# Projecting the samples' queries ahead of the prompt in a one-core decoder step with a streamed key and value cache

## What is computed

```python
qkv = rms_norm(x) @ w_in                       # 1024 -> 3072 = 24 tiles of 128 columns
qa, ka, va, qb, kb, vb = split(qkv)            # 4 tiles each; rope on qa, ka, qb, kb
oa = (softmax(q1 k1^T) - lam * softmax(q2 k2^T)) v      # 4 heads, whole past
ob = dilated_window_attention(qb, kb, vb)               # 8 heads, last 2048 positions
x  = x + concat(headnorm(oa), ob) @ w_out
x  = x + (silu(h @ w_gate) * (h @ w_up)) @ w_down       # h = rms_norm(x)
```

## Time and profile before

| | us |
|---|---|
| median of 3 runs | 1069.75 |
| lowest, highest | 1060.89, 1073.51 |
| the profiled execution | 1071.72 |
| its span | 1070.0 |
| PE busy | 948.3 (89%) |
| DVE busy | 667.0 (62%) |
| ACT busy | 516.6 (48%) |
| POOL busy | 287.7 (27%) |
| moved by DMA | 310.99 MB, mean 291 GB/s |

### The profile page before, as it was taken

How to read it: one execution, slowest core, us unless ns; L and a number is a source line. 1 busy time by engine, 2 the same in 40 slices (tenths; PEclk the granted TensorE clock), 3 DMA queues, 4 the chain that set the end, 5 groups by cost and what they waited for, 6 DMA issues and landing times.

```text
span 1070.0 us, 29358 instructions
## 1 busy us (share of the span) xinstructions
PE 948.3 (89%) x11042; PEld 844.3 (79%) x11042; DVE 667.0 (62%) x1632; ACT 516.6 (48%) x1128; POOL 287.7 (27%) x351
## 2 busy tenths in 40 slices
PE   3989999899977888888898568899999999999996
PEld 2978888788855656676676444899999999999996
DVE  5289845676569997863546355888888888700004
ACT  6554433375236468664242653555555555611124
POOL 1322155555433355335454000000000000233330
PEclk8989999999999999998999868999999999999998
DMA  7789999999999999899988974487686876974632
GB/s 227 270 293 327 350 321 378 365 369 374 381 366 385 370 382 347 275 337 337 357 268 265 304 217 161 162 309 279 243 317 261 310 276 233 338 252 161 230 140 89
DMA packets 158229, 310.99 MB, mean 291 GB/s; under 512 B 14049, under 2 KB 88162, under 8 KB 157090
## 3 DMA queue, kind: packets, MB, share of 16 engines
q1 hardware_dynamic: 134242, 233.92, 63.0%
q0 software_dynamic: 22144, 72.37, 19.1%
q10 hardware_dynamic: 1728, 3.15, 0.9%
HBM read 302.31 MB, written 73.92 MB: 352 GB/s over the span
## 4 chain that ended last, share of the span: by engine, by line
PE 38%; issue 32%; DMA 15%; DVE 6%; ACT 5%; POOL 2%; POOLq 1%; ACTq 0%; SPq 0%; DVEq 0%
DMA v_ring<-in_cache_v_diff 12%; PE ps L1477 11%; PE ps L1111 9%; PE ps L1342 5%; PE ps L1305 4%; PE ps L1262 2%; DVE kt_sb L2280 1%; DMA v_ring<-in_state_v_win 1%; ACT rot L1616 1%; POOL v_ring L698 1%; PE ps L1318 1%; PE ps L1359 1%; PE ps L1188 1%; DMA x<-in_x_prompt 1%; DMA k_ring<-in_cache_k_diff 1%
## 5 line engine op out<-in xcount | busy, mean ns | idle before, releaser
L2280 DVE STREAM_TRANSPOSE kt_sb<-k_ring 128x512 f32<-128x512 f32 x336 | 218.7, 688 | 67.7 <-DMA k_ring<-in_cache_k_diff 30.7
L698 POOL DMA_DIRECT2D v_ring<-in_cache_v_diff x248 | 136.3, 551 | 157.6 <-issue 84.5
L1050 POOL TENSOR_TENSOR c_lo<-c_raw,c_hi 128x1408 fp32r<-128x1408 f32 x14 | 46.6, 3331 | 410.7 <-ACT c_hi L1893 410.7
L1111 PE MATMUL ps<-h_hi,w_hi 128*128 128x288 f32 x384 | 124.8, 325 | 1.9 <-DVE h_lo L2134 1.9
L1111 PE MATMUL ps<-h_lo,w_hi 128*128 128x288 f32 x384 | 115.8, 301 | 0.0
L1342 PE MATMUL ps<-v_ring,pt_sb 128*32 128x128 f32 x2240 | 79.2, 283 | 40.8 <-DMA v_ring<-in_cache_v_diff 34.0
L1111 PE MATMUL ps<-h_hi,w_lo 128*128 128x288 f32 x384 | 115.3, 300 | 0.0
L1342 PEld LDWEIGHTS ps<-v_ring,pt_sb 128*32 128x32 f32 x2240 | 61.1, 113 | 53.2 <-issue 49.5
L1305 PE MATMUL ps<-kt_sb,q_st 128*32 128x128 f32 (+1 forms) x2816 | 95.4, 278 | 6.2 <-DVE q_st L2290 4.1
L1006 POOL TENSOR_TENSOR w_lo<-w_raw,w_hi 128x1024 fp32r<-128x1024 f32 x24 | 57.4, 2392 | 153.7 <-ACT w_hi L1594 153.7
L1305 PEld LDWEIGHTS ps<-kt_sb,q_st 128*32 128x32 f32 x2816 | 72.0, 113 | 23.1 <-issue 16.2
(11 more groups left out here) (249 smaller groups left out, 2346.9 us busy)
## 6 DMA issues: line engine op xcount, KB each, us to landing
k_ring<-in_cache_k_diff SPq DMA_DIRECT2D x256, 256.0 KB, 7.1
v_ring<-in_cache_v_diff POOLq DMA_DIRECT2D x248, 256.0 KB, 7.0
out_k_win_sample<-in_state_k_win SPq DMA_DIRECT2D x32, 1020.0 KB, 8.2
out_v_win_sample<-in_state_v_win SPq DMA_DIRECT2D x32, 1020.0 KB, 8.2
k_ring<-in_state_k_win SPq DMA_DIRECT2D x32, 512.0 KB, 6.7
w_raw<-in_w_in SPq DMA_DIRECT2D x24, 512.0 KB, 7.3
g_raw<-in_w_gate SPq DMA_DIRECT2D x11, 1024.0 KB, 5.4
g_raw<-in_w_up SPq DMA_DIRECT2D x11, 1024.0 KB, 5.4
```

The costliest lines, as they stand in the source:

```text
L698: queue.dma_start(dst, src.rearrange("(b j) c -> j b c", b=4))\
L1050: nc.gpsimd.tensor_tensor(c_lo[j][:, 0:width], c_raw[:, j, 0:width], c_hi[j][:, 0:width].bitcast(F32), ALU.subtract).then_inc(w_lo_done, 1)
L1111: last = nc.tensor.matmul(M[c][:, 0:HALF], wt, act[:, k, c * HALF:(c + 1) * HALF], start=k == 0 and at_first, stop=k == KT - 1 and act is ...
L2280: V.transpose(kt_sb[:, i, :], k_ring[:, i, :]).then_inc(kt_done, 1)
```

## The change

- The samples' block is normalised first (`NORM_ORDER = (4, 0, 1, 2, 3)`). ACT copies its transposed rows to a new buffer `h_s` in plain f32, and `project_samples` multiplies the loaded, unsplit tiles 0 to 3 with it: 8 matmuls of 64 columns a tile into one bank. Tile 3 gets a place of its own (`early_raw`), so that four tiles are loaded at the start.
- `copy_sample_queries` (ACT) and `rope_sample_queries` (DVE) make `q_s` of them; `fetch_first_q` and `fetch_q(0)` run at once, between the norms of the blocks. Tiles 0 to 3 have 2 times 256 columns later on in place of 2 times 288, and their rope leaves the samples out.
- `PRE = 0`: every piece of the prompt is in the groups. `SHARE` is 9 a group for groups 0 to 7 (before: 6), 8 for 8 to 21 (as before), 92 pieces in groups 22 to 37 (before 80), and 4 a group for 38 to 47.
- The page numbers are loaded ahead of the weight tiles and are waited for by themselves; the prompt's blocks of x are loaded by ACT's queue. Item 3 uses place 0 with all of `fetch_q(3)` at the end of group 23.
- The four copies of sample 0 go from tiles 0 to 3 into the down projection's loop.
- Some semaphores are merged; what they order stays.

```diff
-PRE = 36
+PRE = 0
-SHARE = [6] * 8 + [8] * 14 + [5] * 20 + [4, 4] + [3] * 4 + [0] * (SLOTS - 48)
+SHARE = ([9] * 8 + [8] * 14 + [6] * 4 + [5] + [6] * 5 + [7] + [5, 5, 6] + [5, 5] + [4] * 10
+         + [0] * (SLOTS - 48))
-    return 0 if it < 3 else it % 2
-FETCH_AT = {23: 3, 30: 4, 33: 5, 36: 6, 39: 7}
+    return 0 if it < 4 else (it + 1) % 2
+FETCH_AT = {30: 4, 33: 5, 36: 6, 39: 7}
@@ SP
-            for blk in range(NBLK):
-                load_x(blk)
...
-            w_in_chunk(0)
-            w_in_chunk(1)
-            w_in_chunk(2)
+            load_x(4)
+            sp.dma_start(g_rows[:, :], ins["norm_attn_g"].partition_broadcast(P)).then_inc(norm_in[0], 16)
+            sp.dma_start(ident[:, :], consts[:, C_ID:C_ID + P]).then_inc(norm_in[0], 16)
+            sp.dma_start(page_ids[:, :], ...).then_inc(norm_in[0], 16)
+            for n in range(4):
+                w_in_chunk(n)
...
+            sp.wait_ge(norm_in[0], 48)
+            for i in range(8):
+                load_keys(0, i)
...
-                    if j == 4 and n < COPIES:
-                        shift_window(*shifts.pop(0))
...
+                if m % 2:
+                    shift_window("k_win", 0, m // 2)
@@ PE
+            def project_samples(n):
+                pe.wait_ge(*landing_of(n))
+                pe.wait_ge(qs_copied, 2)
+                for k in range(KT):
+                    last = nc.tensor.matmul(Z[1][:, n * NS:n * NS + NS], raw_at(n)[:, k * P:k * P + P], h_s[:, k, :],
+                                            start=k == 0, stop=k == KT - 1)
+                last.then_inc(qs_projected, 1)
...
+            norm_transposes(0, NORM_ORDER[0])
+            for n in range(4):
+                project_samples(n)
+            for u in range(1, NBLK):
+                norm_transposes(u, NORM_ORDER[u])
             pe.wait_ge(hlo_done, 2 * NBLK)
-            for p in range(PRE):
-                main(p)
@@ ACT
+            for blk in range(4):
+                act.dma_start(x[0:P, blk, :], x_of(blk)).then_inc(x_in[blk], 16)
+            squares_of(0)
+            norm_root(0, NORM_ORDER[0])
+            act.wait_ge(xn_t, 1)
+            ... (h_s copies)
+            norm_hi(0, NORM_ORDER[0], h_hi)
             split_hi(0)
+            squares_of(1)
+            norm_root(1, NORM_ORDER[1])
+            squares_of(2)
+            norm_root(2, NORM_ORDER[2])
+            copy_sample_queries()
+            squares_of(3)
+            norm_root(3, NORM_ORDER[3])
+            norm_hi(1, NORM_ORDER[1], h_hi)
+            fetch_q(0)
+            squares_of(4)
+            norm_root(4, NORM_ORDER[4])
+            norm_hi(2, NORM_ORDER[2], h_hi)
+            norm_hi(3, NORM_ORDER[3], h_hi)
+            norm_hi(4, NORM_ORDER[4], h_hi)
@@ DVE
+            def rope_sample_queries():
+                dve.wait_ge(const_in, 16 * N_CONST)
+                dve.wait_ge(qs_copied, 4)
+                for f in range(4):
+                    s = slice(f * NS, f * NS + NS)
+                    V.tensor_tensor(feat[:, 1, s], feat[:, 1, s], rope_cs[:, 0, SEQ:NT], ALU.mult)
+                    last = V.tensor_tensor(rot[:, s], rot[:, s], rope_cs[:, 1, SEQ:NT], ALU.mult)
+                last.then_inc(rope_parts, 2)
+                dve.wait_ge(rope_parts, 2)
+                for f in range(4):
+                    V.tensor_tensor(q_s[:, f, :], feat[:, 1, s], rot[:, s], ALU.add).then_inc(rope_s_done, 1)
...
+                rows(2)
+                rope_sample_queries()
+                fetch_first_q()
+                mean(3)
+                low(1)
+                rows(3)
+                mean(4)
+                low(2)
+                rows(4)
+                low(3)
+                low(4)
```

More of the change, by code:

```diff
@@ L855, in load_values @@
                 values_of_group(sp, t, h, first_ids)
-            sp.wait_ge(const_in, 16 * N_CONST)
-            for i in range(8):
-                load_keys(0, i)
             def store_k(n):
@@ L892, in main @@
                 if p < 8 * TILES:
-                    if j == 0 and n and n + 2 < TILES:
+                    if j == 0 and n >= 2 and n + 2 < TILES:
                         w_in_chunk(n + 2)
@@ L1087, in norm_transposes @@
                 pe.wait_ge(xn_done, u + 1)
-                if u < NBLK and blk >= 3:
+                if 3 <= u < NBLK:
                     pe.wait_ge(hlo_done, 2 * (u - 2))
@@ L1419, in turn_output @@
                 nc.tensor.transpose(X[:, 0:P], o_row[:, :], ident[:, :]).then_inc(x_full, 1)
-            pe.wait_ge(norm_in[0], 32)
-            for blk in range(NBLK):
-                norm_transposes(blk, blk)
+            pe.wait_ge(norm_in[0], 48)
+            norm_transposes(0, NORM_ORDER[0])
[3 more added lines that the diff above has]
+                norm_transposes(u, NORM_ORDER[u])
             pe.wait_ge(hlo_done, 2 * NBLK)
-            for p in range(PRE):
-                main(p)
             pe.wait_ge(const_in, 16 * N_CONST)
@@ L1615, in rotate_halves, with copy_sample_queries @@
                     d = slice(32 * (q ^ 1), 32 * (q ^ 1) + 32)
-                    last = nc.scalar.activation(rot[d, :], feat[s, n % 2, :], ACT.Copy)
+                    last = nc.scalar.activation(rot[d, cols], feat[s, n % 2, cols], ACT.Copy)
                 last.then_inc(rot_done, 1)
+            def copy_sample_queries():
+                act.wait_ge(qs_projected, 4)
+                cols = slice(0, 4 * NS)
+                nc.scalar.activation(feat[:, 1, cols], Z[1][:, cols], ACT.Copy).then_inc(qs_copied, 1)
+                act.wait_ge(qs_copied, 3)
+                for q in range(4):
+                    s = slice(32 * q, 32 * q + 32)
+                    d = slice(32 * (q ^ 1), 32 * (q ^ 1) + 32)
+                    last = nc.scalar.activation(rot[d, cols], feat[s, 1, cols], ACT.Copy)
+                last.then_inc(qs_copied, 1)
             def evac_tokens(n):
@@ L1918, in _ @@
                         main(p)
-                    if (t, i) == (0, 2):
-                        fetch_q(0)
-                    if i == 7 and t + 1 in FIRST[1:3]:
+                    if i == 7 and t + 1 in FIRST[1:4]:
                         fetch_q(FIRST.index(t + 1))
@@ L2135, in norm_lo, with mean, rows, low @@
                                     hi[s].bitcast(F32), ALU.subtract).then_inc(hlo_done, 1)
-            def norm_blocks():
-                for blk in range(NBLK):
-                    norm_mean(blk, blk)
-                    if blk:
-                        norm_rows(blk - 1, blk - 1)
-                norm_lo(0, 0, h_hi, h_lo)
-                norm_rows(NBLK - 1, NBLK - 1)
-                for blk in range(1, NBLK):
-                    norm_lo(blk, blk, h_hi, h_lo)
+            def rope_sample_queries():
[8 more added lines that the diff above has]
+                for f in range(4):
+                    s = slice(f * NS, f * NS + NS)
+                    V.tensor_tensor(q_s[:, f, :], feat[:, 1, s], rot[:, s], ALU.add).then_inc(rope_s_done, 1)
+            def norm_blocks():
+                def mean(u):
+                    norm_mean(u, NORM_ORDER[u])
+                def rows(u):
+                    norm_rows(u, NORM_ORDER[u])
+                def low(u):
+                    norm_lo(u, NORM_ORDER[u], h_hi, h_lo)
+                mean(0)
+                dve.wait_ge(norm_in[0], 48)
+                rows(0)
+                low(0)
+                mean(1)
+                rows(1)
+                mean(2)
+                rows(2)
[9 more added lines that the diff above has]
+                low(4)
             def rope(n):
```

142 lines of the change are left out of this document (77 added, 65 removed).

## The result

| | before | changed |
|---|---|---|
| median, us | 1068.8 (4 runs) | 1098.76 (4 runs) |
| lowest, highest | 1060.89, 1073.51 | 1092.96, 1100.14 |
| span of the profiled execution | 1070.0 | 1097.5 |

The ratio is 1.0289, 95% interval 1.0238 to 1.0341: 30 us slower, where 1065 was forecast and 1079 was the upper end.

The account below looks back on a forecast made before the run. Nearly everything is full from 60 to 130 us, DMA to 600, PE alone from 660. At group 8's first scores +13.1 - 12.3 - 8.9, then +3.2 for owed bytes, make -4.9: 1065 us forecast, range 1052 to 1079.

Parts of the forecast that it names:

- the edits costed at nothing: Sample 0's moved copies, item 3's fetch, the list behind group 22, load issues, merged semaphores, last norm: 0 in the sum.
- Term 1: Start: pieces wait for all five blocks and the samples' chain, first piece from 25.63 to about 38.7, +13.1 us.
- The later bound: Start of the pieces at 42.7 if constants and tile 3 come 4 us later than summed.
- The constants: Start: last constants landed at 23.4 us, and DVE's rope of the samples' queries comes after them.
- Terms 2 and 3: Ahead of group 8: fewer and smaller pieces, -12.3 us, and fewer stalls, -8.9 us.
- Twelve pieces fewer: Ahead of group 8's first scores: 75 pieces instead of 87 with PRE = 0, -9.5 us.
- the 9.8 expected: Groups 0 to 7: expected at 9.8 us a group with a DMA share near 0.9.
- the change of item: Among the stalls before group 8: copies and then scores at 125 us, about 2 us, expected to stay.
- Term 4: Full DMA stage from group 8: 1.18 MB of weights and stores still owed, +3.2 us, bounds 0 and 3.8.
- The pace: Groups 8 to 21: expected at 13.2 to 13.4 us a group.
- B: Rival: PE and DVE take turns in groups 0 to 7, stalls stay at 13, +9 us, 1079; chance 0.16.
- C: Rival: bytes set the end, the full stage gives the earlier start all back, sum 0, 1070; chance 0.12.

Follow-up runs that it names:

- e13_list: Kernel before with the changed kernel's list of pieces, keeping its own start, copies and fetches: 1097.2 us, ratio 1.0302.
- e1: Changed kernel with before's list from group 22 on and the 12 pieces put into groups 8 to 19: 1083.4 us, ratio 1.0104.
- e9: Changed kernel with 52 pieces in groups 22 to 29, reaching before's 236 pieces at group 30, then 5 a group: 1082.6 us, ratio 1.0115.
- e8_spread: Changed kernel with its pieces from group 30 on spread evenly, 5 a group and then 4: 1094.1 us, ratio 1.0252.
- e14_ahead: Kernel before with five more pieces done by group 27, so the attention stands one group earlier from 30 to 36: 1077.2 us, ratio 1.0116.
- e16_both: Changed kernel with 60 warming matmuls at the start and a list reaching 236 pieces at group 30: 1086.3 us, ratio 1.0183.
- e7_copies: Kernel before with only sample 0's four copies moved into the down loop: 1067.9 us, ratio 1.0007.
- e4_pre36: Changed kernel with 36 pieces ahead of the groups (PRE = 36) and before's list: 1085.4 us, ratio 1.0141.
- e6_front: Changed kernel with before's list from group 22 and second place, 18 warming matmuls, blocks' transposes between samples' products, rotation and fetches behind norms: 1071.4 us, ratio 1.0037.
- e2_place: Changed kernel with before's list from group 22, 12 pieces in groups 8 to 19, item 3's second place and copies over group 23: 1078.8 us, ratio 1.0103.
- e3_quarter: Changed kernel with the samples' product doing 2 of 8 depth blocks a tile (wrong first queries): 1094.1 us, ratio 1.0224.

## Why the prediction was wrong

**The step that failed** stands under the edits costed at nothing: "From group 22 on the list makes up its 12 pieces over 16 groups, under the same DMA share." Put at 0, it costs half of the loss or more: alone in the kernel before it makes 1.0302, 30 us (e13_list), and taken out of the changed kernel in two ways it gives 15 to 16 us back by the medians, 19 to 20 by the ratios (e1, e9). What the runs show in its place is groups 30 to 36 in 91.3 us instead of 74.6, at a DMA share of 0.77 for 0.95. It rested on a mean DMA share, 0.96 for 440 to 600 us, which seemed to leave PE (135 busy of 160 us) room. That share depended on the pieces' work falling where PE still used the values in time: it is 0.86 in the changed kernel, and in the six groups of e13_list, the kernel before with another list, 0.79 for 0.95. Counting pieces missed it: e8_spread and e14_ahead have before's number a group there and are slow.

**Term 1**, +13.1, was +21.5 (47.12 instead of 25.63). The samples' product ended at 28.6, not 20.8. I read "x12" as 12 matmuls; in plain f32 each is two instructions, so a tile's 8 are 16. I charged only the last tile's and held the others hidden behind the weights, while 64 at 0.213 us outlast the loads by far. The later bound I gave was 42.7. What came behind the product was sized well: 18.5 us to the first piece, where the sum has 17.9. The constants, at 23.4 in the sum, did not matter: DVE's rope waited for ACT until 30.86. (The first key load, issued at 18.6 instead of 23.47, no longer waits for them.) By the Trainium skill, TensorE: Matmul & The Clock Gate, Part 1, the idle state is the throttled one; the trace agrees with its 0.213 us beside a column of 1.00, against 0.112 in e16_both. Over all 64 instructions the difference is 6.5 us, not 0.4.

**Terms 2 and 3**, -21.2 together, were -17.9: from the first piece to group 8 took 104.7 us before and 86.8 now. The size is near, the parts are less so. Twelve pieces fewer, put at -9.5, brought 3.7 us in the kernel before (e13_list), where a key load stands in the chain; how much of the rest is stalls was not measured apart. Groups 4 to 6 took 10.0 us each for the 9.8 expected, but group 7, with the change of item, 15.4. In the term the change of item is 2 us; it leaves out that PE now waits for the samples' new keys, whose tile is roped just ahead (timeline; before, PE does not wait there):

```profile
122.98 0.32 PE L1313 MATMUL ps<-k_s,q_nat 128*32 128x64 f32 x8 [2.38 <-DVE kT L2255]
```

Group 8 stood at 134.0, not 122.2, 7.8 of it from the product.

**Term 4**, +3.2, was +5.8 from group 8 to 22, inside what two executions differ by. Its bytes are right: up to its group 8 the changed kernel had moved 32.6 MB (134.0 us at 243 GB/s), e7_copies, the kernel before without the four copies, 33.7 (130.0 us at 259), so 1.1 MB were owed for 1.18. The pace, 13.3 us a group, was as forecast. PE was no idle engine there: it is busy 94% from 130 to 300 us, and 9 tenths or more in eight of the page's ten slices from 27 to 294 us, not only from 660.

**The rivals.** B (1079) had the sign but not the mechanism: groups 0 to 7 took 10.2 us in the mean, under the 10.4 from which it was to decide. C, that the full stage gives an early start back, is not what the runs show between kernels with the same list. Before and e4_pre36 stand 17.6 us apart at group 8, 16.5 at group 22 and 17.5 in the median; e6_front and e2_place 9.8, 7.3 and 7.5 (7 by the ratios); e3_quarter and changed 7.9, 11.1 and 4.6. What goes is a lead that was won by leaving pieces to the stage: e1_share's over e4_pre36, 12.3 us at group 8, is 4.8 at group 22, and e6_front's over before, 6.4, is 6.8 behind there, each with 12 pieces more to do in groups 8 to 19. From group 8 to 22 every kernel moved 65.7 to 68.0 MB, at 349 to 368 GB/s, whenever it began: the stage takes its time late as well as early.

With the list mended the changed front costs 11 to 15 us (e1, e2, e9), and with its order mended too, 3 (e6_front). So of the 30 us half (by the ratios two thirds) is given back by mending the list and nearly all the rest by the start; but e13_list, with before's start, loses all 30 by the list alone. The two do not add, and why is open.

## What to carry to other kernels

Where a hand-made list interleaves a long dependent chain with streaming groups, treat the place of each step as tuned: a shift forward by one group cost 10 us, a list up to 12 pieces behind 30 (the kernel before with that list). Test a list alone, in the old kernel, before it is bundled with other edits. Time won ahead of a stage that is full of DMA counts as far as the work left for the stage is the same: with the same list 8 to 18 us at its start were 7 to 17 at its end, but a lead won by leaving 12 pieces to it mostly went. A small product's instructions are to be counted as the trace counts them, at the clock that their spacing shows.
